# Splitting the first reduction group of a fused two-layer mixer kernel in two, and moving loads and a square

## The reference

```python
mod = silu(c) @ w_ada + b_ada                 # w_ada: 2048 x 6144
shift, scale, gate = split(mod, 3)
h = rmsnorm(x, norm_pre) * (1 + scale) + shift
z = h @ w_in                                  # 2048 x 14336, in 7 kinds of columns
y_conv = gb * causal_dwconv3(gc * u) * silu(g_c)
y_ret  = groupnorm(retention(rope(q), rope(k), v)) * silu(g_r)
o = concat(y_conv, y_ret) @ w_out             # 4096 x 2048
x = x + gate * rmsnorm(o, norm_post)
```

## Time and profile before

| | |
|---|---|
| median of 3 runs | 1703.98 us (1703.96 to 1705.44) |
| profiled execution | 1703.92 us, of which the span (first to last instruction) is 1702.1 |
| TensorE busy in the span | 98% |
| VectorE, ScalarE busy | 69%, 43% |
| first product of chunk 0 starts | 26.80 us into the span |

### The profile page before, as it was taken

How to read it: one execution, slowest core, us unless ns; L and a number is a source line. 1 busy time by engine, 2 the same in 40 slices (tenths; PEclk the granted TensorE clock), 3 DMA queues, 4 the chain that set the end, 5 groups by cost and what they waited for, 6 DMA issues and landing times.

```text
span 1702.1 us, 19027 instructions
## 1 busy us (share of the span) xinstructions
PE 1673.7 (98%) x7707; PEld 1370.8 (81%) x7707; DVE 1169.3 (69%) x1325; ACT 733.5 (43%) x817; POOL 52.7 (3%) x94
## 2 busy tenths in 40 slices
PE   6999999999999999999999999999999999999998
PEld 4677788888888888888878888888888888888886
DVE  2578768788678778788886455556645555578777
ACT  4454434534434444344464444344344444444442
POOL 4000000000000000000000000000000000000000
PEclk9999999999999999999999999999999999999999
DMA  9999765897798788888865665566556756678884
GB/s 341 383 374 352 232 206 185 289 305 276 238 310 279 257 300 305 306 282 285 290 198 197 198 222 190 186 193 222 182 183 204 222 187 188 207 263 299 286 289 177
DMA packets 233655, 429.25 MB, mean 252 GB/s; under 512 B 8664, under 2 KB 50024, under 8 KB 232800
## 3 DMA queue, kind: packets, MB, share of 16 engines
q1 hardware_dynamic: 225888, 408.97, 70.3%
q10 hardware_dynamic: 7680, 19.07, 4.2%
HBM read 417.57 MB, written 2.10 MB: 247 GB/s over the span
## 4 chain that ended last, share of the span: by engine, by line
PE 94%; DMA 3%; DVE 1%; ACT 1%; issue 0%; SPq 0%; POOL 0%; DVEq 0%; ACTq 0%
PE Z L1397 30%; PE Z L1399 30%; PE Z L1398 30%; DMA stage<-in_w_in 2%; PE A L1436 1%; PE A L1485 1%; PE B L1485 0%; DMA xt<-in_x 0%; PE A L1578 0%; PE B L1592 0%; PE B L1591 0%; PE B L1590 0%; PE A L1449 0%; DVE xt L1028 0%; DVE w_lo L884 0%
## 5 line engine op out<-in xcount | busy, mean ns | idle before, releaser
L648 ACT CAST w_hi<-stage 128x1024 fp32r<-128x1024 f32 x574 | 602.4, 1052 | 926.6 <-PE Z L1399 838.2
L884 DVE TENSOR_TENSOR w_lo<-stage,w_hi 128x1024 fp32r<-128x1024 f32 x574 | 697.0, 1223 | 439.5 <-ACT w_hi L648 435.5
L1397 PE MATMUL Z<-w_hi,H 128*128 128x512 f32 x1784 | 702.3, 394 | 1.7 <-DVE part L1134 1.7
L1399 PE MATMUL Z<-w_hi,H 128*128 128x512 f32 x1784 | 695.1, 390 | 0.0
L1398 PE MATMUL Z<-w_lo,H 128*128 128x512 f32 x1784 | 694.5, 389 | 0.0
L1397 PEld LDWEIGHTS Z<-w_hi,H 128*128 128x128 f32 x1784 | 335.0, 188 | 77.6 <-issue 5.9
L1399 PEld LDWEIGHTS Z<-w_hi,H 128*128 128x128 f32 x1784 | 334.9, 188 | 70.7
L1398 PEld LDWEIGHTS Z<-w_lo,H 128*128 128x128 f32 x1784 | 335.2, 188 | 67.8
L905 DVE SCALAR_TENSOR_TENSOR acc<-stage,c_silu,acc 128x512 f32<-128x512 f32 x240 | 180.2, 751 | 6.8
L1397 PE MATMUL Z<-w_hi,YC 128*128 128x512 f32 x256 | 100.1, 391 | 0.0
L1397 PE MATMUL Z<-w_hi,YR 128*128 128x512 f32 x256 | 99.9, 390 | 0.0
(11 more groups left out here) (178 smaller groups left out, 740.7 us busy)
## 6 DMA issues: line engine op xcount, KB each, us to landing
stage<-in_w_in SPq DMA_DIRECT2D x186, 1024.0 KB, 5.2
stage<-in_w_ada SPq DMA_DIRECT2D x64, 1024.0 KB, 5.4
stage<-in_w_out SPq DMA_DIRECT2D x64, 1024.0 KB, 5.4
stage<-in_w_in SPq DMA_DIRECT2D x74, 512.0 KB, 4.7
front_stage<-in_w_ada SPq DMA_DIRECT2D x24, 1024.0 KB, 10.9
front_last_stage<-in_w_ada SPq DMA_DIRECT2D x8, 1024.0 KB, 13.1
behind<-R ACTq DMA_DIRECT2D x14, 448.0 KB, 3.5
taps<-in_conv_w ACTq DMA_DIRECT2D x18, 256.0 KB, 6.3
```

The source lines that it names most:

```text
L648: N.copy(w_bufs(n, h)[0], stage[:, slot_of(n), 2 * h:2 * h + 2, :]).then_inc(s_hi, 1)
L884: V.tensor_tensor(lo, stage[:, slot_of(n), 2 * h:2 * h + 2, :], hi.bitcast(F32), ALU.subtract)\
L1397: T.matmul(z[:, i, :], hh, wh, start=ch.first and a == 0, stop=False)
L1399: ins = T.matmul(z[:, i, :], hl, wh, start=False, stop=stop)
```

## The change

Group 0 of two K tiles becomes two groups of one K tile. All later groups and their chunks keep their content but get new numbers: the old chunk n, from 7 on, is n + 7, and the vectors k of the old groups 1 to 4 are k + 2. The conditioning pieces of the new groups 0 and 1 are 1 MiB each, one for each vector, with rows of 128 columns.

In the new group 1 the order of blocks is GG, GB, QK, VV, GR, GC, UU. GG and GB end group 0, and their sums stay in the PSUM banks and go on with group 1 (`HELD`), after which ScalarE copies them. The other five are copied after group 0 and added to after group 1. `EARLY` still follows the group that ends with K tile 3.

The conditioning of the now third group (K tiles 2 and 3) is loaded piece by piece behind chunks 5, 7, 9 and 11. That of K tiles 4 to 7, scale, is loaded behind chunks 13 and 15, where n + 7 would be 14 and 16.

At the start VectorE squares the second token tile with a multiply that sums, ScalarE the first only, and ScalarE runs one silu on a zeroed column ahead of it. The warming matmuls are five. The sines come one group later.

```diff
-FRONT_GROUPS = ((0, 2), (2, 2), (4, 4), (8, 4), (12, 4))
+FRONT_GROUPS = ((0, 1), (1, 1), (2, 2), (4, 4), (8, 4), (12, 4))
-EARLY, EARLY_AFTER = (QK, VV, GR), 1
+EARLY, EARLY_AFTER = (QK, VV, GR), 2
+HELD = (GG, GB)
...
     for g, (k0, tiles) in enumerate(FRONT_GROUPS):
-        for b in range(BLOCKS):
-            table.append(Chunk(False, 0, 0, b, g, q, True, True, k0, tiles // 2))
+        every = HELD + tuple(range(HELD[0])) if g == 1 else range(BLOCKS)
+        for at, b in enumerate(every):
+            table.append(Chunk(False, 0, 0, b, g, q, g != 1 or b not in HELD, g != 0 or b not in HELD, k0, tiles, at))
             q += 1
...
-FRONT_LOAD = {2: 2, 4: 2, 7: 2, 9: 2, 11: 2, 14: 2, 16: 2, 18: 2, 21: 2, 22: 2, 24: 2, 25: 2, 28: 2, 29: 2}
+FRONT_LOAD = {1: 1, 2: 1, 5: 1, 7: 1, 9: 1, 11: 1, 13: 2, 15: 2, 18: 2, 21: 2, 23: 2, 25: 2, 28: 2, 29: 2, 31: 2, 32: 2, 35: 2, 36: 2}
...
-FRONT_USE = {1: ((2, 0), (2, 1)), 3: ((3, 0), (3, 1)), 7: ((4, 0), (4, 1)), 9: ((4, 2), (4, 3)),
-             12: ((5, 0), (5, 1)), 14: ((5, 2), (5, 3))}
-for n, k in ((17, 6), (24, 8)):
+FRONT_USE = {1: ((2, 0),), 2: ((3, 0),), 8: ((4, 0), (4, 1)), 10: ((5, 0), (5, 1)), 14: ((6, 0), (6, 1)), 16: ((6, 2), (6, 3)),
+             19: ((7, 0), (7, 1)), 21: ((7, 2), (7, 3))}
+for n, k in ((24, 8), (31, 10)):
...
-FRONT_ROW = {2: 2, 4: 3, 10: 4, 15: 5, 20: 6, 21: 7, 27: 8, 28: 9}
-FRONT_SUM = {2: 2, 4: 3, 10: 4, 21: 7, 28: 9}
-FRONT_SUM_AMID = {15: 5, 21: 6, 28: 8}
-FRONT_MOD = {3: (2,), 5: (3,), 11: (4,), 16: (5,), 22: (6, 7), 29: (8, 9)}
-FRONT_H = {6: 1, 23: 3, 30: 4}
-FRONT_H_AMID = {17: 2}
+FRONT_ROW = {2: 2, 3: 3, 9: 4, 11: 5, 17: 6, 22: 7, 27: 8, 28: 9, 34: 10, 35: 11}
+FRONT_SUM = {2: 2, 3: 3, 9: 4, 11: 5, 17: 6, 28: 9, 35: 11}
+FRONT_SUM_AMID = {22: 7, 28: 8, 35: 10}
+FRONT_MOD = {3: (2,), 4: (3,), 10: (4,), 12: (5,), 18: (6,), 23: (7,), 29: (8, 9), 36: (10, 11)}
+FRONT_H = {5: 1, 13: 2, 30: 4, 37: 5}
+FRONT_H_AMID = {24: 3}
...
+            act.wait_ge(s_zeros, 1)
+            N.activation(nb4[:, 0:1], c_cols[:, KT - 1, COL - 1:COL], ACT.Silu)
             act.wait_ge(s_x, 32)
-            for i in range(NT):
-                N.activation(part[:, 2 * i:2 * i + 2, :, :].rearrange("p a b c -> p (a b c)"), xt[:, i, :], ACT.Square,
-                             accum_out=xsq[:, i:i + 1]).then_inc(s_xsq, 1)
+            N.activation(part[:, 0:2, :, :].rearrange("p a b c -> p (a b c)"), xt[:, 0, :], ACT.Square,
+                         accum_out=xsq[:, 0:1]).then_inc(s_xsq, 1)
...
             V.memset(c_cols[:, :, :], 0.0).then_inc(s_zeros, 1)
+            dve.wait_ge(s_x, 32)
+            V.tensor_tensor_reduce(part[:, 2:4, :, :].rearrange("p a b c -> p (a b c)"), xt[:, 1, :], xt[:, 1, :], 1.0, 0.0,
+                                   ALU.mult, ALU.add, xsq[:, 1:2]).then_inc(s_xsq, 1)
...
-            bridge(Z[0][:, 0, :], 8)
+            bridge(Z[0][:, 0, :], 5)
```

More of the change, by code:

```diff
@@ L55, with halves @@
 PRM = 272
-FRONT_GROUPS = ((0, 2), (2, 2), (4, 4), (8, 4), (12, 4))
+FRONT_GROUPS = ((0, 1), (1, 1), (2, 2), (4, 4), (8, 4), (12, 4))
 LAST_GROUP = len(FRONT_GROUPS) - 1
-EARLY, EARLY_AFTER = (QK, VV, GR), 1
-Chunk = namedtuple("Chunk", "out l j b g q first last k0 halves")
+EARLY, EARLY_AFTER = (QK, VV, GR), 2
+HELD = (GG, GB)
+Chunk = namedtuple("Chunk", "out l j b g q first last k0 tiles at")
+def halves(c):
+    return -(-c.tiles // 2)
 def chunk_table():
@@ L79, in chunk_table @@
             for b in EARLY:
-                table.append(Chunk(False, 0, 1, b, 0, q, True, True, 0, 2))
+                table.append(Chunk(False, 0, 1, b, 0, q, True, True, 0, CK, 0))
                 q += 1
@@ L86, in chunk_table @@
                 for g in range(start, GROUPS):
-                    table.append(Chunk(False, l, j, b, g, q, g == start, g == GROUPS - 1, CK * g, 2))
+                    table.append(Chunk(False, l, j, b, g, q, g == start, g == GROUPS - 1, CK * g, CK, b))
                 q += 1
@@ L99 @@
 FRONT = len(FRONT_GROUPS) * BLOCKS + len(EARLY)
-HALVES = [sum(c.halves for c in CH[:n]) for n in range(len(CH) + 1)]
+HALVES = [sum(halves(c) for c in CH[:n]) for n in range(len(CH) + 1)]
 SPILL = 2
@@ L109 @@
 for c in CH[:FRONT]:
-    if c.g == 0:
+    if not c.last:
+        continue
+    if (c.j, c.b) not in PART_NO:
         PART_NO[c.j, c.b] = len(PART_NO) + 1
@@ L465, in taken, with added, copied @@
             return z_free(block_no(t, b))
+        def added(n):
+            return CH[n].j == 0 and (CH[n].g, CH[n].b) in FIN_NO
+        def copied(n):
+            return CH[n].last and not added(n)
         def fin(b):
@@ L554, in unit_tiles, with halves_of, half_tiles @@
         def unit_tiles(half):
-            return range(4) if half is None else range(2 * half, 2 * half + 2)
+            return range(4) if half is None else range(2 * half, 2 * half + 2) if half < 2 else range(half - 2, half - 1)
+        def halves_of(k0, tiles):
+            if tiles == 1:
+                return [(k0 // CK, 2 + k0 % CK)]
+            return [(k // CK, k % CK // 2) for k in range(k0, k0 + tiles, 2)]
+        def half_tiles(n, h):
+            return min(2, CH[n].tiles - 2 * h)
         def tokens(i):
@@ L672, in h_full @@
             def h_full(l, k0, tiles):
-                for k in range(k0, k0 + tiles, 2):
-                    h_unit(l, k // 4, k % 4 // 2, None)
+                for g, half in halves_of(k0, tiles):
+                    h_unit(l, g, half, None)
             def x_scaled(g):
@@ L751, in _ @@
                     cast(n, 0)
-                if 0 <= n - SPILL < FRONT and CH[n - SPILL].g == 0:
+                if 0 <= n - SPILL < FRONT and copied(n - SPILL):
                     was = CH[n - SPILL]
@@ L1375, in z_wait @@
                 was = CH[ch.q - 2]
-                if ch.q - 2 < FRONT and was.g == 0:
+                if ch.q - 2 < FRONT and copied(ch.q - 2):
                     pe.wait_ge(s_part, PART_NO[was.j, was.b])
@@ L1386, in products @@
                 z = Z[ch.q % 2]
-                for a in (2 * h, 2 * h + 1):
+                for a in range(2 * h, 2 * h + half_tiles(n, h)):
                     k = ch.k0 + a
@@ L1395, in products @@
                     wh, wl = hi[:, a % 2, :], lo[:, a % 2, :]
[L1396 removed]
+                    stop = ch.last and a == ch.tiles - 1
                     T.matmul(z[:, i, :], hh, wh, start=ch.first and a == 0, stop=False)
@@ L1511, in _ @@
                     z_wait(n)
[L1512 to L1515, removed]
+                    for h in range(halves(ch)):
+                        if not ch.out and ch.at == 0 and ch.j == 0:
+                            g, half = halves_of(ch.k0, ch.tiles)[h]
+                            pe.wait_ge(s_h, UNIT[ch.l, g, half, None] + 1)
                         if ch.out and ch.j == 0 and h == 0:
```

47 lines of the change are left out of this document (25 added, 22 removed).

## The result

The changed kernel takes 1710.31 us (median of 6 runs, 1709.18 to 1710.69) against 1704.03 us (6 runs), a ratio of 1.0033 with a 95% interval of 1.0023 to 1.0043: slower by 6.3 us, 0.37%. The time lies inside the forecast range by 0.2 us, but the case that I held likeliest, +2.8 us and "same", did not come; "slower" did, at 0.40. The profiled execution took 1709.20 us, 5.28 us more than the profiled one of before (spans 1707.4 and 1702.1), so the traces explain 5.3 of the 6.3 us.

What follows compares the result with a forecast made beforehand. The load stream was taken to bound the front up to 73.01 us, with no byte less to load; 512-byte packets (+2.3 us) and chunk 14's later load put chunk 19 2.8 us late: 1703.9 + 2.8 = 1706.7 us, range 1703.0 to 1710.5.

Steps and rivals of the forecast that it cites:

- rival of half pace: TensorE restarts at half clock after the stall ahead of chunk 14, adding 1.7 us: 1708.4 us; chance 18%.
- dear packets: Rival: 512-byte packets cost far more than 28.2 ns; at 37 ns 1711.4 us, at the upper bound 1716.2; chance 10%.
- It holds, by less than 3 us: Load queue: the load after chunk 18 waits for a use at 60.1 us, while the stream gets there at some 63.
- a sign of being wrong: Next profile: a slice of the DMA column under 0.9 before 70 us would mean the load queue ran dry.
- TensorE starts it at 56.4: Chunk 14: its load lands at 54.1 us, cast and split take 2.3, then TensorE starts it.
- 56.4 + 19.4 = 75.8: Start of chunk 19: chunk 14's start plus gapless TensorE work; 2.8 us later than 73.01.
- where chunk 12 could have started: Kernel before: chunk 12's start less its stall, 73.01 - 1.70 = 71.31 us; the end point for the 19.4 us of work.
- 24.5 us of work: TensorE's work from first product to chunk 14, against 36 us until it lands; the rest is stalls.
- the early start: First product: conditioning of 2 MiB instead of 4 lets products start 5 to 6.5 us early, hidden by the load stream.
- nothing is won back or lost again: After chunk 19: old chunk 15 had 3.9 us of slack, while the load moves 2.3 and TensorE 2.8.
- Free packets: Rival: small packets cost nothing, chunk 14's chain ends at 73.5 us, 1704.4 us; chance 26%, together with cheap packets.
- The start carries through: Rival: all after the first product comes 5 to 6.5 us early, 1698 us; needs chunk 19 landed by 64; chance 8%.

Runs made afterwards that it cites:

- e3: Kernel before, with each of the first four conditioning MiB read as two loads of 128 columns (512-byte packets); 1706.36 us, ratio 1.0012.
- e1: Changed kernel, with the two pairs of conditioning loads behind chunks 14 and 16 instead of 13 and 15; 1708.15 us, ratio 1.0021 to the kernel before.
- e2: Kernel before, with only x squared on two engines and the early silu taken from the change; 1703.97 us, ratio 0.9998.
- e8: Changed kernel without held blocks, GG and GB of group 1 starting anew and added by VectorE; 1710.25 us, ratio 1.0032 to the kernel before.
- e6: Kernel before, with half of the four conditioning pieces of K tiles 0 and 1 left out (2 MiB less); 1700.15 us, ratio 0.9974.
- e7: Kernel before, with the conditioning load pair behind chunk 11 moved behind chunk 12 and vector 4's reduction an iteration later; 1703.69 us, ratio 0.9998.
- e5: Kernel of e1, with half of the four conditioning pieces of K tiles 0 and 1 left out (2 MiB less); 1704.33 us, ratio 1.0001 to the kernel before.
- e10: Kernel of e1, with the load pair behind chunk 19, the reduction at 19 and chunk 24's second cast early; 1706.76 us, ratio 1.0017 to the kernel before.
- e9: Kernel of e7, with ScalarE casting the second half of chunk 17's weights right after the first; 1702.60 us, ratio 0.9991 to the kernel before.
- e4: Kernel before, with VectorE doing the add of chunk 10 ahead of the split of chunk 12; 1703.60 us, ratio 0.9995.

## Why the prediction was right or wrong

**Right.** In the kernel before the stream, not the first product, sets the front, and the change moves no byte out of its way. The packets cost 28.3 ns against 28.2, 2.35 us against 2.3 (e3). The order of the conditioning loads is the second loss (e1). The square, the held blocks and the earlier table load count nothing (e2, e8). The first product came early and was waited away.

**Luck: the range.** The measured 1710.31 is 3.6 us above the forecast 1706.7 and 0.2 under the end of the range. That end stood above the rival of half pace (1708.4) and short of that of dear packets (1711.4), neither of which came. What filled the gap was in no rival.

**Wrong: "It holds, by less than 3 us".** The queue did run dry, which the prediction had named as a sign of being wrong. The load behind chunk 18 was issued at 62.28, not 60.1, after the use behind chunk 14, and the DMA share fell to 0.74 for a microsecond. At 154 GB/s in place of 388 this is some 0.6 us of stream, most of the 0.8 by which the load of chunk 19 missed the forecast (cast at 72.58 for 71.8). It stayed hidden, as chunk 19 was held by the chain from chunk 14.

```profile
50.47 6.95 SPq L652 DMA_DIRECT2D stage<-in_w_in  x3
...
62.28 1.23 SPq L628 DMA_DIRECT2D front_stage<-in_w_ada  x2
```

```profile
56.00:60.00 4.00, 1.79 (x8) 1.49 (x9) 4.00 (x4) 1.94 (x3) 0.00 (x0) 1.00 1.05 388
60.00:64.00 4.00, 4.00 (x26) 1.95 (x25) 0.52 (x2) 1.05 (x1) 0.00 (x0) 1.00 0.96 323
63.00:64.00 1.00, 1.00 (x8) 0.85 (x5) 0.10 (x1) 0.87 (x1) 0.00 (x0) 1.00 0.74 154
```

**Wrong: the start of chunk 14**, "TensorE starts it at 56.4", and the sum built on it, "56.4 + 19.4 = 75.8". Measured 58.21 and 78.29. The 2.5 us are four terms. The load landed 0.6 late (cast at 54.72 for 54.1). The add of chunk 12 behind chunk 14's split, 1.2 us, was left out, although the same chain had been read and counted 3.5 us at chunk 12. TensorE's work was 19.53 for 19.38, 0.15. And 71.31, "where chunk 12 could have started", was not a real point: behind a sum over partitions VectorE's reduction, split and add end 0.55 us later than TensorE, in the changed kernel, e1, e6 and e8 alike, hidden in before under the 1.70. The 1.2 alone, which the rows of before already held, would have made the sum 77.0 and the forecast +4.0, slower. Why the load landed 0.6 late was not traced.

**Wrong: the work ahead of chunk 14**, "24.5 us of work", taken from the kernel before, and the adds, judged hidden because VectorE was busy for 23.6 us of 46.2. TensorE worked 28.92 us there, and VectorE's load is not even: ahead of chunk 14 it has 1.9 us for each chunk where TensorE has 1.5. With the loads in the better order (e1) chunk 14 still starts at 56.22, practically the 56.4 that the prediction had put down to its load. The load alone therefore explains only the last 2.0 us.

**Wrong: the early start**, 3.84 us in place of 5 to 6.5. Ten warming matmuls took 3.93 us where sixteen took 3.62 before: TensorE was at half pace until 23 us. H was complete at 21.89 (its low part, L970, starts at 21.39 and takes 0.50), and the warming matmuls held chunk 0 for another 1.1 us. That narrower pieces are the reason for the half pace is likely, but no run tests it. It cost nothing here. Together with 4.45 us more TensorE work up to chunk 14 (conditioning matmuls 6.0 us of busy time against 4.1, as those of one more group now fall into this stretch; the rest in more transposes and in twice as many chunk changes, whose first two products stand 0.3 us apart and the others 0.23), the early start is used up even without a stall.

**Wrong: "nothing is won back or lost again".** For this change it held. As a rule of the kernel it did not: at chunk 17 a gain of 1.7 us was lost in full (e7). The slack was read at chunk 15 and taken for the whole.

**The rivals.** Free packets is out (e3: 286 to 290 GB/s). Dear packets is out by the same run. The start carries through is out by the result, and e5 shows that it would be even with less to load. Half pace at chunk 14 did not appear in either profile of this kernel: behind 3.1 us of idleness the products stand 0.23 us apart from the second on. The Trainium skill, "DMA: Bandwidth & Descriptors", "Why small descriptors are slow (HBM only)", has the direction right, but the estimate from its 3 cycles for each packet was +1.0 us, and e3 measured 2.35: the measurement decides.

**The sum.** Of the 5.3 us between the profiles, 2.0 are the order of the loads (e1), and 3.3 remain. Two chains end there almost together. The stream's: the load of chunk 19 lands 2.9 us late (72.38 for 69.51), of which e3 gives 2.35 to the packets; the thin stretch from 44 to 48 us (307 GB/s for 380, worth some 0.8) can hold the rest, which no run shows. And chunk 14's, which ends 0.4 later still. In e1 chunk 14 starts 4.3 us later than the old chunk 7 (56.22 for 51.93): chunk 0 starts 4.3 earlier (22.50), TensorE works 4.4 longer (28.89 us for 24.47) and stands 4.2 longer (4.83 for 0.66), and 2.94 of that standing is ahead of chunks 12, 13 and 14, where VectorE is the bound. So the stream is not the whole of it: with it moved out of the way (e10) only 1.4 us go, and with the same moves on both sides the new front is still 4.2 us slower. No experiment takes TensorE's added work or VectorE's chain away alone, so what each is worth by itself stays open. The last 1 us, between the growth of the median and of the profiled executions, is open too.

## What to carry to other kernels

Before a start is made earlier, add up the bytes that must land ahead of the first point where the load stream ends last; if the change moves none, the early start is waited away, and finer pieces bring shorter packets, more work and a shallower queue. Look at the cost of one piece on every engine: with half the K tiles TensorE's time for a chunk halved, but VectorE's add did not (1.22 us at either size). An early start counts only once nothing later is waited for (e9). Carry a chain to its end at every point where it is used: the operation that releases the buffer may stand behind the one that was counted. A slack read at one chunk is not the slack of the next; look for the engine with the longest list between two of its own deliveries.

## What the runs showed of the hardware

Halving the packet from 1 KB to 512 bytes took the 16 DMA engines from 348 GB/s to between 286 and 290, and 4 MiB came 2.35 us later (e3). TensorE's pace in the first 23 us changed, while the granted clock read 1.00 in every window: in the changed kernel 32 conditioning matmuls of 128 columns took 1.94 us at 13.43 and again at 16.77, but 1.08 at 26.01, near the ratio of its two levels, 1.2 and 2.4 GHz. Nor was the pace the same wherever the code was: 16 conditioning matmuls of 256 columns took 1.07 us at 19.57 in the kernel before and 1.93 at 20.16 in e4, whose instructions up to there are the same, and the first product came 1.6 us later. A stall of 3.1 us between products later on left the pace as it was.
